# Second layer's q scaled inside its softmax, and its convolution, rotations and attention reordered on TensorE

## The chip, the cores and the metric

The kernel runs on one core of a Trainium2 chip. The metric is device time in microseconds (us) of one execution. A core has TensorE (PE, with its weight loads shown as PEld), VectorE (DVE), ScalarE (ACT), GpSimd (POOL), and the queue from which SyncE issues transfers (SP). Each engine works through its own list in order; semaphores tie the lists together.

## The reference, cut to what matters

Two transformer-like layers on 256 tokens of width 1024. The first has a recurrent unit, sparse attention and a dense feed-forward. The second, which the change touches, has differential attention and a long convolution side by side, then sixteen experts:

```python
q, k, v, hy, gts = jnp.split(proj, splits, axis=-1)        # 4 heads x 2 maps x 64
q = rope_partial(rms_norm_2(q, q_norm_g[li]), cos, sin)    # norm over each 64, then rotation
k = rope_partial(rms_norm_2(k, k_norm_g[li]), cos, sin)
# per head: pr = softmax(q k^T / 8), a = pr[map 0] - lam * pr[map 1], o = a v
o = rms_norm_2(o, subln_g) * (1.0 - lambda_init)           # norm over 128
# hyena: z = short_conv(hy) part; twice z = gate * (irfft(rfft(z) * spec) + skip * z)
merged = g_attn * (attn @ w_branch_attn) + g_hyena * (hyena @ w_branch_hyena)
x = x + merged @ w_out
x = x + expert_choice_ffn(rms_norm_2(x, norm2_g[li]), ...)  # each expert takes its 32 best tokens
```

The norm of q is a factor per token and per 64 channels. It commutes with the rotation, so it can be applied to the scores instead of to q.

## The kernel before

Activations lie with features on the partitions and the 256 tokens on the free axis; the products of the projections are fp32r products of high and low parts of weights and activations (`dense_split`, L463; `token_split`, L481), three products for each. A unit is a 2 MB block of weights, a half is 256 of its output columns. For each piece of weights (four to a half) ScalarE rounds the high part (`round_half`, L1203) and VectorE subtracts it for the low part (`rest_of_half`, L1589); four pieces have room at a time, so a piece can be rounded once TensorE has used the piece four before it. Thus while TensorE computes one half, ScalarE and VectorE prepare the next one.

The order of the work is written out by hand, once per engine. On TensorE, after the three units of the convolution input (L2 to L2+2): q (unit L2+3), k (L2+4), v (L2+5, token major), the gates (L2+6 to L2+9), with the rest between these halves. The names:

- `head_stats(i)` L517: one fp32 product that gives the mean square of each 64 channels, spread over all partitions, into bank 7. i = 6, 7 are the halves of q, 8, 9 those of k.
- `qk_half` L1394 (ScalarE): square, then the root of the means (`root_of`). `head_norm` L1882 (VectorE): `invert` L1558 (the reciprocal, L1561), product with norm weight and 1/root (L1885), product with the cosine (L1888).
- `rope(i)` L759: the permuting product into bank 7, which `finish_rope(i)` L1890 empties (product with the sine, L1892) before adding.
- `turn_hy` L764, `to_freq` L773, `to_time` L788: transposes of the convolution input, transform (m = 0, 1, two banks each), inverse transform. `multiply(o)` L1905 multiplies by the spectrum on VectorE (L1911 to L1923) for m = 0 and 1 in turn, and empties the two banks.
- attention, eight rounds a (head a // 2, query block a % 2): `att2_scores`, one half of the gates' `dense_split`, `att2_turn`, and for odd a `att2_out` and `sub_stats`. On VectorE `normalise2` L1950 takes the row maxima (L1953, L1954), waits for ScalarE's two exponentials (L1428) and normalises (L1956 to L1959). ScalarE then rounds pieces, empties the gates' bank (L1436), copies the transposed probabilities (L1440), squares the output (L1446) and takes a root (L1157) for the norm over 128; VectorE inverts it and scales (L1978).
- After the eight rounds: the branch products (units L2+10, L2+11), w_out, routing, and the loop of the experts.

In that loop, `expert block` semaphores (L956, L1078) let SP issue the load that refills an expert's slot; there are eight slots, and the first eight loads are issued ahead of it (`free`, L1064).

Of the kernel before, what the change touches and what calls it, by code (L numbers as in the profile page):

```python
# [20 lines left out]
ALU = mybir.AluOpType  # L21
# [3 lines left out]
P = 128  # L25
T = 256
# [96 lines left out]
def two_layers(nc, I, table, cols, out):  # L123
    with ExitStack() as ctx:
# [90 lines left out]
        xscale = small[:, 212:214]  # L215

# [57 lines left out]
        rot2 = area(14872, 512)  # L274
        prob2 = area(15872, 2, T)
# [140 lines left out]
        def _(pe):  # L416
# [356 lines left out]
            def to_freq(o, banks):  # L773

                for t in range(TT):
                    if o == 0:
                        wait_taken(("hy turn", 0, t))
                    else:
                        wait_taken(("hy time", 0, t))
                for m in range(2):  # L780
                    for part in range(2):
                        ps = take(banks[m][part], ("freq", o, m, part))
                        for t in range(TT):
                            c = part * T + m * P
                            last = mm(ps[:, :], fwd[:, t, c:c + P], ztok[:, t, :], t == 0, t == 1)
                        last.then_inc(S("freq"), 1)
# [16 lines left out]
            head_stats(6)  # L803
# [37 lines left out]
            def sub_stats(h):  # L841
                pe.wait_ge(S("out2 squares"), h + 1)
                ps = dense_bank(("sub", h))
                mm(ps[:, 0:T], mean_128, sqr[:, 0, 0:T]).then_inc(S("sub stats"), 1)

            halves = [(n, h) for n in range(L2 + 6, L2 + 10) for h in range(2)]
            for a in range(8):
                att2_scores(a)
                dense_split(*halves[a], 4)
                att2_turn(a)  # L850
                if a == 1:
                    to_freq(1, ((6, 7), (6, 7)))
                if a == 3:
                    to_time(1, (6, 7))
                if a % 2:
                    att2_out(a // 2)
                    sub_stats(a // 2)
# [4 lines left out]
            for h in range(4):  # L862
                wait_taken(("out2", h))
# [233 lines left out]
        def _(act):  # L1097
# [296 lines left out]
            def qk_half(i):  # L1394

                n, h = L2 + 3 + i // 2, i % 2
# [8 lines left out]
            qk_half(0)  # L1405
# [4 lines left out]
            qk_half(1)  # L1410
# [13 lines left out]
            for a in range(8):  # L1424
                h, q = a // 2, a % 2
                act.wait_ge(S("maxima2"), a + 1)
                for m in range(2):
                    ins = A(prob2[:, m, :], ps(("att2", a))[:, m * T:m * T + T], ACT.Exp, bias=nmx[:, m:m + 1],  # L1428
                            scale=SC1, accum_out=rsum[:, m:m + 1])
# [11 lines left out]
                if q:  # L1441
                    act.wait_ge(S("att2 out"), h + 1)
                    act.wait_ge(S("head stats"), 10)
                    if h:
                        act.wait_ge(S("sub stats"), h)
                    A(sqr[:, 0, 0:T], ps(("out2", h))[:, 0:T], ACT.Square).then_inc(S("out2 squares"), 1)  # L1446
                    root_of(("sub", h), T, "sub stats", h + 1)
# [48 lines left out]
        def _(dve):  # L1496
# [385 lines left out]
            def head_norm(i):  # L1882
                n, h = L2 + 3 + i // 2, i % 2
                invert(512, ("heads", 6 + i))
                X.scalar_tensor_tensor(rot, ps((n, h))[:, :], V("qn2" if i < 2 else "kn2"), rstd[:, :],  # L1885
# [4 lines left out]
            def finish_rope(i):  # L1890
                dve.wait_ge(S("rotated"), i + 1)
                empty(X.tensor_tensor(pair(rot), pair(ps(("rope", i))[:, :]), C("sin").unsqueeze(1).broadcast_to([P, 2, T]),  # L1892
                                      ALU.mult), ("rope", i))
                wait_taken(("rope", i))
                if i < 2:
                    X.tensor_tensor(q2[:, 2 * i:2 * i + 2, :], pair(rot), pair(rot2), ALU.add).then_inc(S("heads roped"), 1)
# [8 lines left out]
            def multiply(o):  # L1905

                for m in range(2):
                    zc, zs = ps(("freq", o, m, 0)), ps(("freq", o, m, 1))
                    pc, pz = spec[:, o, m, :], spec[:, o, 2 + m, :]
                    dve.wait_ge(S("freq"), 4 * o + 2 * m + 2)  # L1910
                    X.tensor_tensor(ya[:, m, :], zc[:, :], pc, ALU.mult)  # L1911
                    empty(X.tensor_tensor(ya[:, 2 + m, :], zc[:, :], pz, ALU.mult), ("freq", o, m, 0))
                    X.tensor_tensor(cross[:, 0, :], zs[:, :], pz, ALU.mult)
                    empty(X.tensor_tensor(cross[:, 1, :], zs[:, :], pc, ALU.mult), ("freq", o, m, 1))
                    wait_taken(("freq", o, m, 0))
                    wait_taken(("freq", o, m, 1))
                    minus = row0[:, 1:2] if m == 0 else -1.0
                    link(X.scalar_tensor_tensor(ya[:, m, :], cross[:, 0, :], minus, ya[:, m, :], ALU.mult, ALU.add))
                    link(X.tensor_tensor(ya[:, 2 + m, :], ya[:, 2 + m, :], cross[:, 1, :], ALU.add))
                    if m == 0:  # L1920
                        X.tensor_copy(ya[0:1, 2, :], cross[0:1, 0, :]).then_inc(S("products"), 1)
                    else:
                        X.tensor_copy(cross[:, 1, 0:8], cross[:, 0, 0:8]).then_inc(S("products"), 1)  # L1923
                    dve.wait_ge(S("products"), 2 * o + m + 1)

            rest_of_half(LATE + 15)
            head_norm(0)
# [22 lines left out]
            def normalise2(a):  # L1950
                h, q = a // 2, a % 2
                dve.wait_ge(S("att2 scores"), a + 1)
                link(X.tensor_reduce(mx[:, 0:2], pair(ps(("att2", a))[:, :]), AX.X, ALU.max))  # L1953
# [196 lines left out]
```

## Time and profile before

| | us |
|---|---|
| median of 3 runs | 1250.22 (1246.04 to 1253.16) |
| the profiled execution | 1249.02 |
| its span in the trace | 1247.1 |
| PE busy, of the span | 1136.6 (91%) |
| DVE busy | 509.0 (41%) |
| ACT busy | 399.1 (32%) |
| granted TensorE clock, mean | 0.969 |

The span is cut by the trace into a first layer and the inputs of the second (to 566), the stretch that the change rewrites (566.6 to 711.6), the branch products (to 739.4), w_out and routing (to 786) and the experts (to 1236), with a short end. A busy share of 91% says only that TensorE always has a product open; what a change is worth is read in its own stretch, from the time TensorE sat idle there, and from what the stages behind it wait for. In a line of the timeline the number in brackets is the idle time of the engine just before, and what ended it. Some starts of products overlap the modelled end of the one ahead, so a step is best read from start to start.

### The profile page before, as it was taken

To read this page: it belongs to the slowest core of one execution; us is meant where nothing else is said; L and a number is where in the kernel's file an instruction comes from. 1 tells how busy PE (TensorE), PEld (TensorE's weight loads), DVE (VectorE), ACT (ScalarE), POOL (GpSimd) and SP (SyncE) were. 2 spreads that over 40 slices of the span, in tenths; PEclk is the share of its full clock that TensorE was granted. 3 is DMA by queue.
4 is the path that set the end of the run, shared out by engine and by line. 5 is a ranking of instruction groups with operands and counts; after the bars stand their busy time and mean duration, and the time that the engine had idled before them with its cause. 6 is when DMAs were issued, how large, how long until landed. Compare 5 with 4: busy or idle time off the path is not lost.

```text
span 1247.1 us, 16271 instructions
## 1 busy us (share of the span) xinstructions
PE 1136.6 (91%) x6529; PEld 797.5 (64%) x6529; DVE 509.0 (41%) x970; ACT 399.1 (32%) x760; POOL 16.3 (1%) x28
## 2 busy tenths in 40 slices
PE   6999999999999999898899998798888887889886
PEld 5778989877899999896568887323232332323231
DVE  3357776585566655678856522200100010001001
ACT  2251665934656444564245602000000000000000
POOL 3000000000000000000000000000000000000000
PEclk8899999999999999899999999799999999999998
DMA  7163543333344667354122584499999999999997
GB/s 220 68 211 135 169 150 127 114 135 136 136 174 164 181 169 189 135 173 143 65 94 69 214 356 169 185 429 428 428 428 428 429 429 429 429 428 428 428 424 277
DMA packets 94059, 309.31 MB, mean 248 GB/s; under 512 B 6000, under 2 KB 39032, under 8 KB 82040
## 3 DMA queue, kind: packets, MB, share of 16 engines
q1 hardware_dynamic: 93256, 307.42, 64.0%
q0 software_dynamic: 496, 1.07, 0.4%
q8 instruction: 36, 0.59, 0.2%
q10 hardware_dynamic: 256, 0.10, 0.0%
q14 instruction: 15, 0.12, 0.0%
HBM read 307.53 MB, written 1.05 MB: 247 GB/s over the span
## 4 chain that ended last, share of the span: by engine, by line
PE 66%; DMA 26%; DVE 5%; ACT 1%; issue 1%; SPq 0%; ACTq 0%; DVEq 0%
PE bank L431 65%; DMA arena<-in_w_up 17%; DMA arena<-in_w_down 9%; DVE rstd L1561 1%; DVE parts L1589 1%; PE bank L638 0%; DMA arena<-in_x 0%; DVE arena L1524 0%; SPq L1084 0%; ACT root L1157 0%; DVE arena L1885 0%; DVE hidden_parts L1796 0%; DVE arena L1888 0%; ACT parts L1203 0%; DVE arena L1911 0%
## 5 line engine op out<-in xcount | busy, mean ns | idle before, releaser
L431 PE MATMUL bank<-arena 128*32 128x512 f32 (+6 forms) x724 | 268.4, 545 | 8.1 <-ACT arena L1492 3.0
L431 PE MATMUL bank<-parts 128*128 128x256 f32 (+1 forms) x1872 | 243.6, 291 | 5.0 <-DVE parts L1603 4.3
L431 PEld LDWEIGHTS bank<-parts 128*128 128x128 f32 x1872 | 232.9, 193 | 19.5 <-issue 16.5
L1589 DVE TENSOR_TENSOR parts<-ring,parts 128x512 fp32r<-128x512 f32 x288 | 193.0, 690 | 116.1 <-ACT parts L1203 114.8
L1203 ACT ACTIVATE parts<-ring 128x512 fp32r<-128x512 f32 x288 | 178.2, 628 | 189.5 <-PE bank L431 188.5
L431 PE MATMUL bank<-parts_room,arena 128*32 128x512 f32 x384 | 170.7, 634 | 20.5 <-DMA arena<-in_w_up 11.2
L431 PE MATMUL bank<-hidden_parts,parts 128*128 128x256 f32 x1024 | 164.9, 283 | 0.0
L431 PEld LDWEIGHTS bank<-hidden_parts,parts 128*128 128x128 f32 x1024 | 141.4, 192 | 0.1
L431 PEld LDWEIGHTS bank<-arena 128*32 128x32 f32 (+3 forms) x724 | 103.9, 174 | 40.2 <-issue 26.0
L2081 DVE TENSOR_TENSOR arena<-bank,arena 128x512 f32<-128x512 f32 x8 | 5.2, 686 | 279.8 <-ACT arena L1488 279.8
L431 PE MATMUL bank<-cst,arena 128*32 128x512 f32 (+2 forms) x226 | 97.0, 583 | 17.6 <-DMA arena<-in_w_gate 8.2
L431 PE MATMUL bank<-xh,arena 128*32 128x512 f32 (+1 forms) x224 | 94.1, 596 | 16.2 <-DMA parts_room<-in_w_up 8.2
L431 PE MATMUL bank<-xh_parts,parts 128*128 128x256 f32 x512 | 92.7, 283 | 0.6 <-DVE hidden_parts L1796 0.5
L431 PEld LDWEIGHTS bank<-parts_room,arena 128*32 128x32 f32 x384 | 39.5, 115 | 78.7 <-issue 72.4
L431 PE MATMUL bank<-ring,arena 128*32 128x512 f32 x384 | 84.7, 593 | 5.0 <-DMA ring<-in_w_gate 5.0
L431 PE MATMUL bank<-xh,ring 128*128 128x256 f32 x352 | 82.9, 397 | 1.3 <-DVE xh L1529 1.3
L431 PEld LDWEIGHTS bank<-xh_parts,parts 128*128 128x128 f32 x512 | 80.0, 192 | 1.0 <-DVE hidden_parts L1796 0.7
L431 PEld LDWEIGHTS bank<-xh,ring 128*128 128x128 f32 x352 | 70.3, 200 | 15.0 <-issue 4.7
L431 PEld LDWEIGHTS bank<-cst,arena 128*32 128x32 f32 (+2 forms) x226 | 26.9, 124 | 75.2 <-issue 73.2
L431 PEld LDWEIGHTS bank<-xh,arena 128*32 128x32 f32 (+1 forms) x224 | 24.3, 118 | 76.4 <-issue 74.0
L431 PEld LDWEIGHTS bank<-ring,arena 128*32 128x32 f32 x384 | 25.0, 110 | 57.3 <-issue 57.0
L1488 ACT ACTIVATE arena<-bank 128x512 f32<-128x512 f32 x8 | 4.3, 594 | 172.1 <-PE bank L431 172.1
(276 smaller groups left out, 925.6 us busy)
## 6 DMA issues: line engine op xcount, KB each, us to landing
ring<-in_w_in SPq DMA_DIRECT2D x22, 2048.0 KB, 7.9
ring<-in_w_gate SPq DMA_DIRECT2D x16, 2048.0 KB, 27.0
parts_room<-in_w_up SPq DMA_DIRECT2D x16, 2048.0 KB, 27.0
ring<-in_w_ff_in SPq DMA_DIRECT2D x8, 2048.0 KB, 8.5
ring<-in_w_ff_out SPq DMA_DIRECT2D x8, 2048.0 KB, 9.0
cst<-in_w_gate SPq DMA_DIRECT2D x8, 2048.0 KB, 22.7
arena<-in_w_gate SPq DMA_DIRECT2D x8, 2048.0 KB, 27.2
xh<-in_w_up SPq DMA_DIRECT2D x8, 2048.0 KB, 25.6
```

Source lines behind the costliest of these rows:

```text
L431: return nc.tensor.matmul(o, lhsT=l, rhs=r, start=first, stop=last)
L1203: A(w_part[0][:, p % PIECES], piece_of(n, p), ACT.Copy).then_inc(S("pieces rounded"), 1)
L1488: A(hs[:, 512 * h:512 * h + 512], bank[h][:, :], ACT.Silu).then_inc(emptied[h], 1)
L1561: X.reciprocal(rstd[:, 0:n], root[:, 0:n]).then_inc(S("rstd"), 1)
L1589: X.tensor_tensor(w_part[1][:, p % PIECES], piece_of(n, p), w_part[0][:, p % PIECES].bitcast(F32), ALU.subtract).then_inc(S("pieces split" ...
L2081: X.tensor_tensor(hh[:, 512 * h:512 * h + 512], bank[2 + h][:, :], hs[:, 512 * h:512 * h + 512], ALU.mult)\
```

## The change

Four things are done:

- **q is not normalised ahead of its rotation.** ScalarE copies q times the norm weight out of the bank (`q_half`), and VectorE's product with 1/root is gone for i = 0, 1. The mean squares of q are formed with tokens on the partitions (`q_stats`: four fp32 products of 2 columns for each half), their roots are 8 columns wide, and their reciprocals, times 1/8, are the scale of the softmax's exponentials and of its maxima.
- **The orders on TensorE** of turns, rotations, statistics and transforms change; `to_freq` and `multiply` are split by m and put at separate places, the last rotation goes behind `to_time(0)`.
- **In attention** the scores of round a + 1 are issued behind the turn of round a, and VectorE takes its maxima behind the pieces of weights of round a.
- **The norm over 128** is done for two heads at once (512 columns), after the fifth round and behind the first branch product; the outputs are first copied out of their banks by ScalarE.

```diff
             def rope(i):
                 wait_taken((L2 + 3 + i // 2, i % 2))
                 ps = take(7, ("rope", i))
-                mm(ps[:, :], C("perm"), rot).then_inc(S("rotated"), 1)
+                mm(ps[:, :], C("perm"), rot_q[:, i, :] if i < 2 else rot).then_inc(S("rotated"), 1)
+
+            def q_stats(i):
+
+                ps = take(7, ("q stats", i))
+                pe.wait_ge(S("head squares"), 7 + i)
+                for h in range(2):
+                    for t in range(TT):
+                        c = h * T + t * P
+                        last = mm(ps[:, 4 * h + 2 * t:4 * h + 2 * t + 2], sqr[:, i % 2, c:c + P], mean_64[:, 0:P:64])
+                last.then_inc(S("head stats"), 1)
...
             dense_split(L2 + 3, 0, 4)
-            head_stats(6)
             turn_hy(0)
             dense_split(L2 + 3, 1, 4)
             rope(0)
-            head_stats(7)
             turn_hy(1)
+            q_stats(0)
             dense_split(L2 + 4, 0, 4)
             rope(1)
+            to_freq(0, 0, (4, 5))
+            q_stats(1)
+            dense_split(L2 + 4, 1, 4)
             head_stats(8)
-            to_freq(0, ((4, 5), (4, 5)))
-            dense_split(L2 + 4, 1, 4)
-            rope(2)
-            head_stats(9)
-            token_split(L2 + 5, 4, lambda: rope(3))
+            to_freq(0, 1, (4, 5))
+
+            def between_values():
+                rope(2)
+                head_stats(9)
+
+            token_split(L2 + 5, 4, between_values)
             to_time(0, (5, 6))
+            rope(3)
 
             def att2_scores(a):
                 h, q = a // 2, a % 2
-                pe.wait_ge(S("heads roped"), 4)
+                pe.wait_ge(S("heads roped"), 3 + h // 2)
...
+            att2_scores(0)
             for a in range(8):
-                att2_scores(a)
                 dense_split(*halves[a], 4)
                 att2_turn(a)
-                if a == 1:
-                    to_freq(1, ((6, 7), (6, 7)))
+                if a < 7:
+                    att2_scores(a + 1)
+                if a % 2:
+                    att2_out(a // 2)
+                if a < 2:
+                    to_freq(1, a, (6, 7))
                 if a == 3:
                     to_time(1, (6, 7))
-                if a % 2:
-                    att2_out(a // 2)
-                    sub_stats(a // 2)
+                if a == 4:
+                    sub_stats(0)
             for t in range(2):
                 wait_taken(("hy time", 1, t))
             for h in range(4):
                 dense(L2 + 10, h, hyo, 4)
-            for h in range(4):
-                wait_taken(("out2", h))
+                if h == 0:
+                    sub_stats(1)
+            pe.wait_ge(S("att normed"), 2)
...
+            def q_half(i):
+
+                n, h = L2 + 3, i
                 act.wait_ge(*done((n, h)))
                 head_square(6 + i, ps((n, h))[:, :])
-                root_of(("heads", 6 + i), 512, "head stats", 7 + i)
+                empty(A(rot_q[:, i, :], ps((n, h))[:, :], ACT.Copy, scale=V("qn2")), (n, h))
+
+            def q_roots(i):
+                act.wait_ge(S("head stats"), 7 + i)
+                empty(A(q_root[:, 8 * i:8 * i + 8], ps(("q stats", i))[:, 0:8], ACT.Sqrt, bias=eps), ("q stats", i))
...
+            q_roots(0)
             round_half(LATE + 17)
-            qk_half(2)
+            k_square(2)
+            q_roots(1)
             round_half(LATE + 18)
-            qk_half(3)
+            k_square(3)
+            root_of(("heads", 8), 512, "head stats", 9)
             round_half(LATE + 19)
+            root_of(("heads", 9), 512, "head stats", 10)
             round_half(LATE + 20)
...
             rest_of_half(LATE + 15)
-            head_norm(0)
+            q_turned_by_cosine(0)
             dve.wait_ge(S("pads set again"), 2)
             rest_of_half(LATE + 16)
             finish_rope(0)
-            head_norm(1)
+            q_turned_by_cosine(1)
             rest_of_half(LATE + 17)
             finish_rope(1)
-            head_norm(2)
...
-            multiply(0)
+            multiply(0, 0)
+            for i in range(2):
+                wait_taken(("q stats", i))
+            link(X.reciprocal(q_scale, q_root))
+            link(X.tensor_scalar(q_scale, q_scale, SC1, None, ALU.mult))
             rest_of_half(LATE + 18)
+            k_norm(2)
+            multiply(0, 1)
+            rest_of_half(LATE + 19)
             finish_rope(2)
-            head_norm(3)
-            rest_of_half(LATE + 19)
-            finish_rope(3)
+            k_norm(3)
             rest_of_half(LATE + 20)
...
+            finish_rope(3)
...
+            maxima2(0)
             for a in range(8):
...
                 normalise2(a)
-                if a < 7:
-                    rest_of_half(LATE + 21 + a)
-                if a == 1:
-                    multiply(1)
-                if a == 3:
+                if a in (1, 2):
+                    multiply(1, a - 1)
+                if a == 4:
...
+                if a < 7:
+                    rest_of_half(LATE + 21 + a)
+                    maxima2(a + 1)
+                if a == 5:
+                    norm_heads(0)
+            norm_heads(1)
```

`k_norm(i)` is the old `head_norm(i)` for k; `q_turned_by_cosine(i)` is its product with the cosine alone. `maxima2` is the first half of the old `normalise2`, with `q_scale` in place of 1/8, and waits for the turn of the round before. `norm_heads(i)` inverts 512 roots and scales two heads in place.

## Rows read from the trace of the kernel before

**Rows 1.** The page: the chain that ended last, shares of the span by engine.

```profile
...
PE 66%; DMA 26%; DVE 5%; ACT 1%; issue 1%; SPq 0%; ACTq 0%; DVEq 0%
...
```

**Rows 2.** SP's queue from 690 us on: who it waited for: us in total, times, longest.

```profile
...
SPq L1084 <- PE bank L431: 431.0, 46, 26.8
...
```

**Rows 3.** Windows: length, busy (instructions) of PE, PEld, DVE, ACT, POOL, clock, DMA share, GB/s.

```profile
...
566.60:711.60 145.00, 129.68 (x745) 101.44 (x745) 98.35 (x157) 63.38 (x126) 0.00 (x0) 0.99 0.30 104
...
817.00:1236.00 419.00, 357.30 (x1599) 129.08 (x1598) 23.70 (x49) 22.47 (x38) 0.00 (x0) 0.96 1.00 426
...
595.90:600.80 4.90, 4.90 (x9) 2.12 (x9) 2.99 (x5) 0.00 (x0) 0.00 (x0) 0.65 0.00 0
...
```

**Rows 4.** TensorE's timeline, q to v: start, us, line, names, shapes, count, idle before.

```profile
...
559.75 6.88 PE L431 MATMUL bank<-parts 128*128 128x256 f32 x56
567.92 1.10 PE L431 MATMUL bank<-sqr,cst 128*128 128x512 f32 x2 [1.30 <-ACT sqr L1166]
568.86 1.04 PE L770 MATMUL bank<-cst,arena 128*128 128x128 f32 x8
569.65 6.00 PE L431 MATMUL bank<-parts 128*128 128x256 f32 x48
575.49 1.02 PE L431 MATMUL bank<-arena,cst 128*128 128x512 f32 x2
...
588.73 3.60 PE L431 MATMUL bank<-arena,cst 128*128 128x512 f32 x8
595.89 5.40 PE L431 MATMUL bank<-arena,cst 128*128 128x512 f32 x8 [3.57 <-DVE arena L1912]
...
616.61 5.76 PE L431 MATMUL bank<-parts 128*128 128x512 f32 x24
...
```

**Rows 5.** TensorE's timeline, attention and behind it.

```profile
...
622.21 7.03 PE L431 MATMUL bank<-arena,cst 128*128 128x512 f32 x16
629.07 1.02 PE L431 MATMUL bank<-arena 128*128 128x512 f32 x2
...
635.68 0.38 PE L829 MATMUL bank<-cst,arena 128*128 128x128 f32 x2
...
692.62 1.13 PE L431 MATMUL bank<-arena 128*128 128x256 f32 x4 [1.26 <-ACT arena L1440]
...
709.49 1.13 PE L431 MATMUL bank<-arena 128*128 128x256 f32 x4 [0.74 <-ACT arena L1440]
...
711.63 27.79 PE L431 MATMUL bank<-arena,ring 128*128 128x256 f32 x128
...
760.27 0.96 PE L431 MATMUL bank<-router,arena 128*128 128x16 f32 x8
...
```

**Rows 6.** VectorE's timeline.

```profile
...
569.78 3.35 DVE L1561 RECIPROCAL rstd<-root 128x512 f32<-128x512 f32 x1 [1.76 <-ACT root L1157]
...
574.68 2.50 DVE L1589 TENSOR_TENSOR parts<-ring,parts 128x512 fp32r<-128x512 f32 x4
...
594.55 0.69 DVE L1911 TENSOR_TENSOR arena<-bank,arena 128x512 f32<-128x512 f32 x1
...
598.65 0.42 DVE L1921 COPY arena<-arena 1x512 f32<-1x512 f32 x1
...
658.02 0.68 DVE L1953 TENSOR_REDUCE small<-bank 128x2 f32<-128x512 f32 x1
...
660.76 0.48 DVE L1959 SCALAR_TENSOR_TENSOR arena<-arena,small 128x256 f32<-128x256 f32 x1
...
```

**Rows 7.** ScalarE's timeline.

```profile
...
567.20 0.58 ACT L1166 ACTIVATE sqr<-bank 128x512 f32<-128x512 f32 x1
569.06 0.69 ACT L1157 ACTIVATE root<-bank,small 128x512 f32<-128x512 f32 x1 [1.28 <-PE bank L431]
...
652.71 1.28 ACT L1157 ACT_TABLE_LOAD   x1
654.00 0.47 ACT L1157 ACTIVATE root<-bank,small 128x256 f32<-128x256 f32 x1
...
```

More of the change, by code:

```diff
@@ L771, in turn_hy, with to_freq @@
                     last.then_inc(S("hy turned"), 1)
-            def to_freq(o, banks):
+            def to_freq(o, m, banks):
                 for t in range(TT):
[L776 to L786, printed above, removed]
+                    wait_taken(("hy turn", 0, t) if o == 0 else ("hy time", 0, t))
+                for part in range(2):
+                    ps = take(banks[part], ("freq", o, m, part))
+                    for t in range(TT):
+                        c = part * T + m * P
+                        last = mm(ps[:, :], fwd[:, t, c:c + P], ztok[:, t, :], t == 0, t == 1)
+                    last.then_inc(S("freq"), 1)
             def to_time(o, banks):
@@ L839, in att2_out, with sub_stats @@
                 last.then_inc(S("att2 out"), 1)
[L841 to L844, printed above, removed]
+            def sub_stats(i):
+                pe.wait_ge(S("out2 squares"), 2 * i + 2)
+                ps = dense_bank(("sub", i))
+                mm(ps[:, :], mean_128, sqr[:, i, :]).then_inc(S("sub stats"), 1)
             halves = [(n, h) for n in range(L2 + 6, L2 + 10) for h in range(2)]
+            att2_scores(0)
             for a in range(8):
-                att2_scores(a)
                 dense_split(*halves[a], 4)
                 att2_turn(a)
-                if a == 1:
-                    to_freq(1, ((6, 7), (6, 7)))
+                if a < 7:
[4 more added lines that the diff above has]
+                    to_freq(1, a, (6, 7))
                 if a == 3:
                     to_time(1, (6, 7))
-                if a % 2:
-                    att2_out(a // 2)
-                    sub_stats(a // 2)
+                if a == 4:
+                    sub_stats(0)
             for t in range(2):
@@ L1443, in _ @@
                     act.wait_ge(S("head stats"), 10)
[L1444 to L1447, printed above, removed]
+                    A(sqr[:, h // 2, (h % 2) * T:(h % 2) * T + T], ps(("out2", h))[:, 0:T], ACT.Square)\
+                        .then_inc(S("out2 squares"), 1)
+                    empty(A(att[:, h, :], ps(("out2", h))[:, 0:T], ACT.Copy), ("out2", h))
+                if a == 4:
+                    root_of(("sub", 0), 512, "sub stats", 1)
+            root_of(("sub", 1), 512, "sub stats", 2)
             for n, gates in ((L2 + 8, gates_h), (L2 + 6, gates_d)):
@@ L1891, in finish_rope @@
                 dve.wait_ge(S("rotated"), i + 1)
-                empty(X.tensor_tensor(pair(rot), pair(ps(("rope", i))[:, :]), C("sin").unsqueeze(1).broadcast_to([P, 2, T]),
+                r = rot_q[:, i, :] if i < 2 else rot
+                empty(X.tensor_tensor(pair(r), pair(ps(("rope", i))[:, :]), C("sin").unsqueeze(1).broadcast_to([P, 2, T]),
                                       ALU.mult), ("rope", i))
@@ L1903, in finish_rope @@
                 dve.wait_ge(S("heads roped"), i + 1)
[L1905 to L1924, printed above, removed]
@@ new lines, in multiply @@
+            def multiply(o, m):
+                zc, zs = ps(("freq", o, m, 0)), ps(("freq", o, m, 1))
+                pc, pz = spec[:, o, m, :], spec[:, o, 2 + m, :]
+                dve.wait_ge(S("freq"), 4 * o + 2 * m + 2)
+                X.tensor_tensor(ya[:, m, :], zc[:, :], pc, ALU.mult)
+                empty(X.tensor_tensor(ya[:, 2 + m, :], zc[:, :], pz, ALU.mult), ("freq", o, m, 0))
+                X.tensor_tensor(cross[:, 0, :], zs[:, :], pz, ALU.mult)
+                empty(X.tensor_tensor(cross[:, 1, :], zs[:, :], pc, ALU.mult), ("freq", o, m, 1))
+                wait_taken(("freq", o, m, 0))
+                wait_taken(("freq", o, m, 1))
+                minus = row0[:, 1:2] if m == 0 else -1.0
+                link(X.scalar_tensor_tensor(ya[:, m, :], cross[:, 0, :], minus, ya[:, m, :], ALU.mult, ALU.add))
+                link(X.tensor_tensor(ya[:, 2 + m, :], ya[:, 2 + m, :], cross[:, 1, :], ALU.add))
+                if m == 0:
+                    X.tensor_copy(ya[0:1, 2, :], cross[0:1, 0, :]).then_inc(S("products"), 1)
+                else:
+                    X.tensor_copy(cross[:, 1, 0:8], cross[:, 0, 0:8]).then_inc(S("products"), 1)
+                dve.wait_ge(S("products"), 2 * o + m + 1)
@@ L1960, in normalise2, with norm_heads @@
                     .then_inc(S("probs2"), 1)
+            def norm_heads(i):
+                invert(512, ("sub", i))
+                for h in (2 * i, 2 * i + 1):
+                    wait_taken(("out2", h))
+                pair_of = att[:, 2 * i:2 * i + 2, :]
+                X.scalar_tensor_tensor(flat(pair_of), flat(pair_of), lam[:, 5:6], rstd[:, :], ALU.mult, ALU.mult)\
+                    .then_inc(S("att normed"), 1)
+            maxima2(0)
             for a in range(8):
-                h, q = a // 2, a % 2
-                if a:
-                    dve.wait_ge(S("probs2 turned"), a)
                 normalise2(a)
-                if a < 7:
-                    rest_of_half(LATE + 21 + a)
-                if a == 1:
-                    multiply(1)
-                if a == 3:
+                if a in (1, 2):
+                    multiply(1, a - 1)
+                if a == 4:
                     for t in range(2):
```

39 lines of the change are left out of this document (23 added, 16 removed).

## The prediction

> **What bounds the kernel now.** First the chain that ended last [rows 1]: 66% of it is TensorE, 26% DMA. The DMA share all lies in the experts: from 817 to 1236 the DMA engines are busy all the time at 426 GB/s [rows 3], with TensorE waiting for them. But this stream has no clock of its own. SP's loads from 690 us on waited 46 times, 431 us in all, for TensorE [rows 2], since a load is issued when an expert block has used its slot. The first eight are ahead of the loop, the rest hang on its first block. So what TensorE saves ahead of the experts moves the stream and the end by as much, until the eight loads ahead become late.
>
> Ahead of the experts TensorE's own list is the bound. The stretch of the change begins where the first half of q ends (559.75 + 6.88 = 566.6 [rows 4]) and ends where the branch products begin, 711.6 [rows 5]: 145.0 us, in which TensorE is busy 129.7 [rows 3] and idle 15.3. This idle time is in a few gaps that the timeline shows with their releasers: 1.30 for the square of q, 3.57 for a bank that `multiply` holds [rows 4], 1.26 and 0.74 for the copies of the turned probabilities [rows 5], and others like them. VectorE and ScalarE are busy 98 and 63 us of the 145 [rows 3]: neither is the bound, but their order decides when a bank comes free.
>
> **The work on TensorE, step by step.** From start to start: a product of 512 fp32 columns 0.86 (eight in 622.21 to 629.07, the inverse transform [rows 5]), 0.95 where it stands alone (567.92 to 568.86 [rows 4]); eight turns 0.8 (to 569.65); a half with pieces 5.85 in q and k (to 575.49 [rows 4]) and 5.75 in attention (629.07 to 635.68 less a score of 0.86 [rows 5]); a half of v 5.7 (616.61 to 622.21 [rows 4, 5]); four products of `to_freq` 3.45. Thus, before: statistics 3.8, turns 1.6, rotations 3.6, `to_freq` 4 x 3.45 = 13.8, three halves 17.5, v 11.4, `to_time` 2 x 6.9 = 13.8, scores 8 x 0.86 = 6.9, gates 46.0, eight turns of 0.22 (an estimate from the eight in 0.8) 1.8, four outputs at 0.95 3.8, four norms of 256 columns at 0.53 (an estimate, half a 512 and a start) 2.1. Sum 126.1. So 145.0 - 126.1 = 18.9 us are not work: 15.3 idle, 1.4 in the second `to_freq` at half clock (below), and 2.2 in seams.
>
> **What is removed or made cheaper.** The q statistics become 8 products of 2 columns. The trace has no such product; the nearest row is the router's, 16 columns, 8 records (4 fp32 products) in 0.96 us [rows 5], where the stationary load is the cost. So four make 0.96 instead of 0.95: nothing. Bounds: 0.5 (only the records' starts) to 1.6 each, -0.9 to +1.3 for both. Two norms of 512 columns instead of four of 256: 1.9 for 2.1, one of them behind 711.6. VectorE loses two inversions of 3.35 [rows 6] and two products, gains two tiny ones; ScalarE has two copies of 0.6 for two roots of 0.7 [rows 7], and in attention two pairs of table loads instead of four.
>
> **The gaps after the change.** I write the lists out with these durations on the clock of the trace of before.
>
> q: the turns follow the first half at once (the 1.30 is gone), the second half runs 567.4 to 573.4, rotation and turns to 575.1. `q_stats(0)` needs bank 7 from `finish_rope(0)`, which is queued on VectorE behind four pieces; these end 1.7 after the half (577.2 against 575.49 [rows 4, 6]), so 575.1, and the sine product makes 575.8. Gap 0.7. k: `q_stats(0)` to 576.8, half to 582.6, rotation 583.5, first `to_freq` 587.0, `q_stats(1)` 587.9, half 593.8, `head_stats(8)` 594.7, second `to_freq` 598.2. Its banks were emptied long before, since `multiply(0, 0)` ran beside: the 3.57 and what hangs on it are gone. The first half of v to 603.9, `rope(2)` to 604.8.
>
> Then `head_stats(9)` needs bank 7 again, and I expect the largest new gap here. VectorE: pieces to 595.4; the root of `head_stats(8)` on ScalarE at 595.8 (behind a piece, the square 0.58 and 0.69 [rows 7]); inversion 3.35 and two products to 600.7; `multiply(0, 1)` 4.5 (594.55 to 599.07 [rows 6]) to 605.3; four pieces 2.5 to 607.8; sine product to 608.5. Gap 3.7. Queued behind this wait on TensorE are the second half of v, `to_time(0)`, all of attention.
>
> The clock: behind the idle 3.57 the granted clock was 0.65 on average in 595.9 to 600.8, where 3.45 us of products took 4.9 [rows 3, 4]; it fell to the 1.2 GHz level for some of it. I take the same 1.4 for the new gap of 3.7. Bounds 0 and 2.5 (half a clock over five us). The Trainium skill, "TensorE: Matmul & The Clock Gate", in "What's actually happening", says that an idle array goes to 1.2 GHz and that the moment varies between runs; by that the 1.4 could be missing in one execution with no change to the kernel. The row of this case shows only that it fell once.
>
> Attention: `rope(3)` and the first score wait for nothing. VectorE takes the maxima of round 0 at 626; softmax takes 3.2 (658.02 to 661.24 [rows 6]), done 1 us before the turn. In each later round the softmax follows TensorE's half by pieces 1.7, maxima 0.9, exponentials 1.1, normalising 1.3 = 5.0, while TensorE has turn, score and half, 6.8. So the turns wait for nothing, except round 6, behind the inversion of 512 (3.35): 0.2. `att2_out` waits for ScalarE's copy behind the gates' bank: 1.26 before in round 5, now less the score that lies in front of it, 0.4, in three rounds; in round 7, with no score, 0.74 [rows 5]. Together 2.0. The waits for the four squares and for `to_freq`'s second half are gone. Cover: were VectorE late, the next wait is that of the turn for the probabilities, at most 1 us away in rounds 0, 5 and 6. The last `norm_heads` ends about 5 us before the attention branch reads it, the gates' sigmoid about 3 us before its first bank is wanted; nothing.
>
> Sum after: gaps 0.7 + 3.7 + 1.4 + 2.0 + 0.2 = 8.0, seams 1.1 (half of 2.2, since half of those lay at banks that are now free; bounds 0.5 and 2.2) = 9.1 us instead of 18.9. With work less by 2.1 - 1.9 = 0.2 up to the end of the branch products (739.4 [rows 5]), they end 10.0 us earlier.
>
> **Does it arrive?** w_out's loads hang on the last gate half and move along; so do routing and the first expert block. 1249.0 (profiled, 1.9 beyond its span) - 10.0 = **1239.0 us**. That execution lies 1.2 under the median shown, so of the median 10 us would make 1240.2; I stay with the profiled one.
>
> **A rule weighed.** The root and the exponentials need different tables. The trace: load 1.28 at 652.71, root at 654.00, no pause [rows 7]. In round 4 the sequence score, `sub_stats`, root, load, exponentials leaves 0.4 us to the turn of round 5. The Trainium skill, "ScalarE: Activation LUTs", in "What ACT_TABLE_LOAD costs", gives 1.38 us of drain to each switch besides; by that the two switches would take 2.8 more, and the time would be 1239.0 + 2.4 = 1241.4. The rows speak against it.
>
> **Rivals.**
> 1. More comes: the gap at `head_stats(9)` stays under that which lowers the clock, seams vanish: 1239.0 - 1.4 - 1.6 = 1236. For it: the gap hangs on a chain of ten durations. Against: 3.57 lowered it once.
> 2. The thin margins break: the turns of rounds 0, 5, 6 and the second half of v each 1.5 late: +6, 1245. For: margins of 1 us and less. Against: each duration is read from a row.
> 3. The stream of the experts doesn't follow, because one of the eight loads ahead lands too late: 1249. Against: SP waited for TensorE 46 times and the DMA engines were idle before the loop.
> 4. The drains of the table loads: 1241.4.
> 5. Slower: the softmax, now behind the pieces of its own round on VectorE, becomes the chain of attention. It costs nothing up to 6.8 us a round. At 9.5 us it costs 8 x 2.7 = 21.6: 1260. It makes the kernel slower than before from 1.25 us a round over 6.8, slower by 0.5% from 2.0. Against: the sum is 5.0; for: a copy of the output and a square stand before the exponentials of even rounds, 5.9.
>
> **How the numbers follow.** Forecast 0.60, rival 1 0.12, rival 2 0.14, rival 3 0.05, rival 4 0.04, rival 5 0.05. The unknown costs reach from 1236 to 1242 in the forecast's own case. The range takes in rivals 1, 2 and 4 and the scatter of the runs (7 us between lowest and highest): 1233 to 1246; out are rivals 3 and 5, 0.10, and tails. A measurement of this kernel tells about 0.5%, 6.2 us, from no change: under 1244.0 counts as faster. Forecast, rivals 1 and 4 and a fifth of rival 2: 0.79. Same: the rest of rival 2, rival 3, a little of 5: 0.17. Slower 0.04.
>
> **What would show it.** In the profile after: no idle time before the turns at 566.6; under 1 us at `q_stats`; none at the second `to_freq`; one gap of 3 to 4 us inside v, released by the sine product, with a lower clock behind it; the branch products begin near 700.6; the first block of the experts 10 us earlier, the stream at the same rate. The prediction is wrong if that gap is over 8 us, or turns in attention wait for the probabilities in most rounds, or the products of 2 columns take over 0.3 us each.

## The result

The changed kernel takes 1236.22 us (median; 1233.94 to 1238.53), the kernel before 1248.95 in the same comparison (1246.04 to 1253.16): ratio 0.9897, 95% interval 0.9874 to 0.9921. That is 12.7 us less where 10.0 were forecast, and 2.8 under the forecast time of 1239.0, inside the range. The profiled execution of the changed kernel is its slowest, 1238.53, with a span of 1236.5; one thing that lengthened it is seen further down.

The page of the changed kernel, busy time and chain:

```profile
span 1236.5 us, 16274 instructions
...
PE 1136.0 (92%) x6537; PEld 800.6 (65%) x6537; DVE 500.8 (41%) x964; ACT 396.7 (32%) x760; POOL 16.3 (1%) x28
...
PE 67%; DMA 27%; DVE 3%; ACT 1%; issue 1%; SPq 0%; ACTq 0%; DVEq 0%
```

Over the whole span TensorE is busy nearly as long as before (1136.0 against 1136.6 us; this includes 2.4 us more in the last eight products, shown below), and VectorE's part of the chain went from 5% [rows 1] to 3%. In the rewritten part, from the end of q's first half to the first branch product, the window reads (length, busy of PE, PEld, DVE, ACT, POOL, granted clock, DMA share, GB/s):

```profile
566.60:698.80 132.20, 126.50 (x751) 101.89 (x750) 88.46 (x151) 59.73 (x123) 0.00 (x0) 0.99 0.32 111
```

TensorE sat idle 5.7 us there (132.2 - 126.5), and 15.3 before [rows 3]: most of what went is waiting. The timeline of TensorE, q to v (start, length, line, names, shapes, count, idle before):

```profile
566.43 1.04 PE L783 MATMUL bank<-cst,arena 128*128 128x128 f32 x8
567.22 6.00 PE L434 MATMUL bank<-parts 128*128 128x256 f32 x48
...
575.27 1.05 PE L434 MATMUL bank<-cst,sqr 128*128 128x2 f32 x8 [0.32 <-DVE arena L1930]
576.18 6.00 PE L434 MATMUL bank<-parts 128*128 128x256 f32 x48
582.02 4.45 PE L434 MATMUL bank<-arena,cst 128*128 128x512 f32 x10
586.31 0.95 PE L434 MATMUL bank<-cst,sqr 128*128 128x2 f32 x8
587.12 6.00 PE L434 MATMUL bank<-parts 128*128 128x256 f32 x48
592.96 1.02 PE L434 MATMUL bank<-sqr,cst 128*128 128x512 f32 x2
593.81 3.60 PE L434 MATMUL bank<-arena,cst 128*128 128x512 f32 x8
596.85 6.05 PE L434 MATMUL bank<-parts 128*128 128x512 f32 x24
602.73 1.02 PE L434 MATMUL bank<-arena,cst 128*128 128x512 f32 x2
607.19 1.83 PE L434 MATMUL bank<-sqr,cst 128*128 128x512 f32 x2 [3.44 <-DVE arena L1930]
608.04 7.38 PE L434 MATMUL bank<-parts 128*128 128x512 f32 x24
615.26 7.89 PE L434 MATMUL bank<-arena,cst 128*128 128x512 f32 x18
```

Against [rows 4]: the 1.30 and its like ahead of the statistics are gone but for 0.32, the second half of the transform (the 3.57 of before) follows without a bracket, and one gap is left, 3.44 us inside v. Attention and the branch products:

```profile
641.49 1.13 PE L434 MATMUL bank<-arena 128*128 128x256 f32 x4 [0.40 <-ACT arena L1471]
...
697.83 1.13 PE L434 MATMUL bank<-arena 128*128 128x256 f32 x4 [0.74 <-ACT arena L1471]
698.80 3.62 PE L434 MATMUL bank<-arena,ring 128*128 128x256 f32 x16
702.25 1.02 PE L434 MATMUL bank<-sqr,cst 128*128 128x512 f32 x2
703.11 24.34 PE L434 MATMUL bank<-arena,ring 128*128 128x256 f32 x112
```

The 0.40 stands in three rounds. I call the time from the end of q's first half to the first branch product the **stretch**. It was 145.0 us (566.6 to 711.6 [rows 4, 5]); it is 132.2 (566.6 to 698.8), 12.8 less. One norm of 0.86 now lies behind its end (702.25 to 703.11), so the branch products end 12.0 earlier, at 727.45 instead of 739.42 [rows 5].

### The profile page after: what moved, and what is told of

Same layout as the page of the kernel before. It is cut to its first block, busy times and chain, and to the rows that moved or that the text cites. A ratio compares the mean times of both kernels' runs of the same rounds, so it can differ in the third digit from the quotient of the medians.

```text
span 1236.5 us, 16274 instructions
## 1 busy us (share of the span) xinstructions
PE 1136.0 (92%) x6537; PEld 800.6 (65%) x6537; DVE 500.8 (41%) x964; ACT 396.7 (32%) x760; POOL 16.3 (1%) x28
## 4 chain that ended last, share of the span: by engine, by line
PE 67%; DMA 27%; DVE 3%; ACT 1%; issue 1%; SPq 0%; ACTq 0%; DVEq 0%
PE bank L434 66%; DMA arena<-in_w_up 17%; DMA arena<-in_w_down 9%; DVE parts L1622 1%; PE bank L641 0%; DVE rstd L1594 0%; DMA arena<-in_x 0%; DVE arena L1557 0%; SPq L1102 0%; DVE hidden_parts L1829 0%; ACT parts L1221 0%; PE bank L547 0%; PE bank L892 0%; ACT arena L1467 0%; DVE arena L2089 0%
```

## The experiments

Each kernel is read in two ways: its time beside the kernel before, with the ratio, and its stretch in the profile, which leaves out what varies ahead of it and behind.

**Which part gives the gain.** First the attention of the kernel before in the changed kernel (short: the lists of the three engines from the first score to the branch products).

```diff
-            att2_scores(0)
             for a in range(8):
+                att2_scores(a)
                 dense_split(*halves[a], 4)
                 att2_turn(a)
-                if a < 7:
-                    att2_scores(a + 1)
...
+                    sub_stats(a // 2)
```

> The changed kernel with the attention stretch of the kernel before: scores, half, turn in one round, all of the transform's second use behind round 1, four norms of 256 columns; q's scale stays in the softmax. Theory (the gain is the sum of TensorE's gaps, place by place, and nothing behind them gives it back): the attention stretch from the first score to the branch products goes back from 76.7 us (75.8 and the norm that lies behind) to 82.6, so 5.9 us more than the changed kernel, about 6 less than before: 1242, ratio 0.995. Rival (q's inversions out of VectorE's list are the gain, the order of attention is worth little): within 2 us of the changed kernel, 1236 to 1238.

Measured: 1247.27 us, ratio 0.9980 (0.9962 to 0.9998), stretch 142.0, so 9.8 more than the changed kernel where 5.9 and the 0.86 of the norm were expected. The timeline of TensorE shows a wait that neither kernel has:

```profile
607.18 1.90 PE L434 MATMUL bank<-sqr,cst 128*128 128x512 f32 x2 [3.43 <-DVE arena L1925]
625.37 1.12 PE L434 MATMUL bank<-arena 128*128 128x512 f32 x2 [2.20 <-DVE arena L1933]
644.20 3.67 PE L434 MATMUL bank<-arena,cst 128*128 128x512 f32 x8 [1.47 <-DVE arena L1944]
```

The old list waits for all four rotations ahead of the first score; the new list of q and k puts the last one behind the inverse transform. So I ran it again with the weaker wait:

```diff
-                pe.wait_ge(S("heads roped"), 4)
+                pe.wait_ge(S("heads roped"), 3 + h // 2)
```

> As the run with the old attention, but the first score waits only for the first half of k, as in the changed kernel. Theory (the 2.2 us by which that run lay beyond the sum of the gaps is a wait of the first score for the second half of k, whose rotation the new order puts behind the inverse transform): from the end of q's first half to the branch products 139.8 us instead of 142.0, no idle time ahead of the first score, and the two parts then add to the whole within 1 us. Rival (the old attention costs more on the new q and k for another reason, such as VectorE's list): 142 again.

Measured: 1242.65 us, ratio 0.9958 (0.9935 to 0.9982), stretch 139.5, no idle time ahead of the first score. The 2.2 us were that wait; the stretch is 2.5 shorter, since a wait costs more than its bracket (see below).

The other way round, the kernel before with the attention of the changed one:

> The kernel before with the attention stretch of the changed kernel only; q is normalised ahead of its rotation and everything up to the first score has the old order. Theory: TensorE's gaps up to the first score stay (8.8 idle and 1.4 of clock), those in attention go: 5.9 us less than before, 1243, ratio 0.995; with the other run the two parts add to the 12 us that the branch products gained. Rival (q's inversions are the gain): under 2 us less than before, ratio above 0.998.

Measured: 1242.17 us, ratio 0.9953 (0.9936 to 0.9969), stretch 138.3 (565.0 to 703.3): 6.8 less than before, of which 0.86 is the norm that lies behind; 5.9 as expected. The parts: 145.0 - 139.5 = 5.5 for q and k, 6.8 for attention, 12.3 of the 12.8 together. The rival falls: half of the gain has nothing to do with q. The place of the scores and the norm over two heads were only tested together.

**What scaling q in the softmax is worth.** The changed order, q normalised ahead of its rotation again:

```diff
             turn_hy(0)
+            head_stats(6)
             dense_split(L2 + 3, 1, 4)
             rope(0)
             turn_hy(1)
-            q_stats(0)
+            head_stats(7)
...
-            q_turned_by_cosine(0)
+            k_norm(0)
```

> The changed kernel's order, but q normalised ahead of its rotation: statistics spread over the partitions behind the turns of either half, root of 512, inversion of 512 and product with 1/root on VectorE, 1/8 alone in the softmax. Theory: VectorE has room for the two inversions in q and k, only the second statistics wait longer for bank 7 (gap 1.6 instead of 0.3): 1.3 to 1.6 us more than the changed kernel, 1238. Rival (the scaling in the softmax is what frees VectorE): 6 us or more above the changed kernel, 1242.

Measured: 1237.44 us (1232.90 to 1241.87), ratio 0.9911 (0.9877 to 0.9944), not to be told from the changed kernel. In its profile:

```profile
577.59 1.12 PE L434 MATMUL bank<-sqr,cst 128*128 128x512 f32 x2 [1.34 <-DVE arena L1929]
...
594.34 1.02 PE L434 MATMUL bank<-sqr,cst 128*128 128x512 f32 x2
...
608.57 1.13 PE L434 MATMUL bank<-sqr,cst 128*128 128x512 f32 x2 [3.43 <-DVE arena L1929]
609.13 6.05 PE L434 MATMUL bank<-parts 128*128 128x512 f32 x24
```

The first k statistics stand 28.0 us behind q's first half (566.4 to 594.3) instead of 26.4 (566.6 to 593.0): the 1.6 expected. But behind the gap of 3.43 the statistics and the second half of v take 6.45 (608.57 to 615.02) where the changed kernel takes 8.07 (607.19 to 615.26), and the stretch is 132.1. What this says of the clock comes below. The two inversions of 3.35 us that left VectorE are worth 1.6 us by the gaps, and in this profile the clock gave just as much back: the order gave the rest.

**What the split of the transform is worth.** Both of its halves behind the k statistics again:

```diff
             rope(1)
-            to_freq(0, 0, (4, 5))
             q_stats(1)
             dense_split(L2 + 4, 1, 4)
             head_stats(8)
+            to_freq(0, 0, (4, 5))
             to_freq(0, 1, (4, 5))
```

> The changed kernel with the first transform in one piece again: both halves of it behind the k statistics, and VectorE's two products behind the first inversion of k. Theory: TensorE waits 5 us at the second half for the banks that VectorE empties behind the inversion, with the clock at half behind it, and the gap at the last k statistics shrinks to 1: 4.4 us more than the changed kernel, 1240.6. Rival (the order within VectorE's list is indifferent, since it is busy 41%): no change.

Measured: 1240.68 us, 4.5 over the changed kernel, ratio 0.9938 (0.9918 to 0.9959); stretch 135.5, 3.3 more. That the medians lie as far apart as was forecast (4.4) is luck in part: by the stretch the forecast was 1.1 too large, since the wait was 3.81 and not 5. It is where it was forecast, with a smaller one at `q_stats(1)` and one at the last statistics (1.19):

```profile
583.02 1.05 PE L434 MATMUL bank<-cst,sqr 128*128 128x2 f32 x8 [1.19 <-DVE arena L1930]
598.03 5.37 PE L434 MATMUL bank<-arena,cst 128*128 128x512 f32 x8 [3.81 <-DVE arena L1949]
```

VectorE is busy 41% of the span, and the order within its list is still worth 3.3 us of the stretch.

**The gap that is left.** The last k statistics in bank 6, so that the sine product isn't waited for:

```diff
-            def head_stats(i, n=512):
+            def head_stats(i, n=512, b=7):
 
-                ps = take(7, ("heads", i))
+                ps = take(b, ("heads", i))
...
                 rope(2)
-                head_stats(9)
+                head_stats(9, b=6)
```

> The changed kernel, the last k statistics in bank 6 instead of bank 7, so that they needn't wait for the sine product. Theory: the gap of 3.44 us inside v shrinks to about 0.25 (the pieces of the second half of v are ready at 604.7), the clock stays at full behind it (1.3 us), and nothing else is late: 4.8 us less than the changed kernel, 1231.4. Rival (the clock's dip has nothing to do with the gap): 3.2 us less and the dip still there. Rival (VectorE's chain is next: the second inversion and the pieces behind it are late): the gap moves behind v and under 1 us is gained.

Measured: 1232.12 us, 4.1 less than the changed kernel by the medians (four executions, two near 1229.5 and two near 1234.8), ratio 0.9876 (0.9829 to 0.9924). The stretch is 127.3 (565.3 to 692.6), 4.9 less, as expected. The gap is 0.17, then:

```profile
603.45 5.73 PE L434 MATMUL bank<-parts 128*128 128x512 f32 x24 [0.17 <-DVE parts L1622]
609.02 7.88 PE L434 MATMUL bank<-arena,cst 128*128 128x512 f32 x18
```

Next, ScalarE's copies in the other order, besides:

```diff
+                act.wait_ge(S("probs2 turned"), a + 1)
+                if q == 0 and h:
+                    act.wait_ge(S("att2 out"), h)
+                empty(A(aT[:, :, q * P:q * P + P], ...), ("turn2", a))
                 act.wait_ge(*done((n, hh_)))
                 dst = (gates_d if a < 4 else gates_h)[:, 2 * (a % 4):2 * (a % 4) + 2, :]
                 empty(A(dst, pair(ps((n, hh_))[:, :]), ACT.Copy), (n, hh_))
```

> The last k statistics in bank 6, and on ScalarE the copy of the turned probabilities ahead of the copy out of the gates' bank. Theory: besides the 4.8 us of bank 6, the waits of the attention outputs go (0.40 in three rounds, and 0.4 of the 0.74 in the last): 6.2 to 6.4 us less than the changed kernel, 1230, which would beat both. Rival (the turn of the next round then waits for the probabilities instead, since their margin in rounds 5 and 6 was 0.3 and 0.1): 4.8 less.

Measured: **1229.86 us** (1228.43 to 1232.29), ratio 0.9853 (0.9808 to 0.9897); stretch 126.1, 6.1 less than the changed kernel. The three waits of 0.40 are gone and the 0.74 is 0.47; in round 6 the turn now waits 0.37 for the probabilities. By its median this version lies 6.4 under the changed kernel and is the fastest here; the run with bank 6 alone is not told from it by its interval, only by the stretch (1.2 longer).

And the sine product ahead of the pieces instead:

```diff
             multiply(0, 1)
-            rest_of_half(LATE + 19)
             finish_rope(2)
+            rest_of_half(LATE + 19)
```

> The changed kernel, with VectorE's sine product and additions of k's first half ahead of the four pieces of weights for the second half of v instead of behind them. Theory: the one gap of 3.44 us becomes two of 1.2 us, ahead of the k statistics and ahead of the second half of v, and the clock does not fall: 2.7 us less than the changed kernel, 1233.5. Rival (the clock goes by the sum of idle time in the stretch): the dip stays, 1.3 less.

Measured: 1235.35 us where 1233.5 was expected, ratio 0.9893 (0.9848 to 0.9938), stretch 131.1, 1.2 less than the changed kernel instead of 2.7. The two gaps came (1.02 each), but the clock fell all the same. TensorE's timeline, and windows (length, busy of PE, PEld, DVE, ACT, POOL, granted clock, DMA share, GB/s):

```profile
606.03 1.13 PE L434 MATMUL bank<-sqr,cst 128*128 128x512 f32 x2 [1.02 <-DVE arena L1930]
608.18 7.36 PE L434 MATMUL bank<-parts 128*128 128x512 f32 x24 [1.02 <-DVE parts L1622]
...
608.00:610.00 2.00, 1.82 (x5) 1.45 (x6) 1.93 (x4) 0.00 (x0) 0.00 (x0) 0.69 0.00 0
610.00:612.00 2.00, 2.00 (x6) 1.60 (x5) 1.98 (x1) 0.63 (x1) 0.00 (x0) 0.50 0.48 65
```

My expectation for the clock failed here; the rival's 1.3 came. The next run asks whether one gap as long as these two together does it too.

```diff
             multiply(0, 1)
+            link(X.reciprocal(cross[:, 0, 0:256]..., mean_d...))
             rest_of_half(LATE + 19)
```

> The run with bank 6 for the last k statistics, and one more reciprocal of 256 columns (1.75 us) on VectorE ahead of the pieces for the second half of v; its result is not used. Theory (idle time makes the clock fall even when it is spread or short of 3 us, as in the run with two gaps of 1.0): one gap of 1.9 us ahead of the second half of v and half clock behind it, 3.0 us more in the stretch than with bank 6 alone, 130.3. Rival (a gap of 1.9 leaves the clock alone, and the other run fell for the product between its gaps): 1.75 more, 129.0, granted clock 1.00 throughout.

Measured: 1236.78 us in one execution, stretch 130.7, 3.4 more than with bank 6 alone, gap 1.96, clock 0.50 behind it:

```profile
606.00:608.00 2.00, 2.00 (x6) 1.55 (x5) 1.97 (x4) 0.34 (x1) 0.00 (x0) 0.50 0.04 9
```

**How much room attention has.** A reciprocal whose result is not used, 1.75 us, ahead of the maxima of each round:

```diff
                     rest_of_half(LATE + 21 + a)
+                    link(X.reciprocal(rot2[:, 0:256]..., mean_d...))
                     maxima2(a + 1)
```

> The changed kernel with one more reciprocal of 256 columns (1.75 us) on VectorE ahead of the maxima in rounds 1 to 7; its result is not used. Theory (margins differ from round to round, and the delays of rounds 1 and 2 add up ahead of the pieces for round 3): 2.2 at the pieces of round 3, 1.4 at its turn, nothing in round 4, 1.5, 1.7 and 0.6 in rounds 5 to 7: 7.4 us more from the first score to the branch products. Rival (the softmax is the chain of every round): 12.3 us more. Rival (VectorE is not near a bound in attention): 0 to 2.

Measured: 1239.67 us in one execution, stretch 136.0, 3.8 more instead of 7.4. TensorE waited for the probabilities in rounds 3, 6 and 7:

```profile
658.69 0.44 PE L843 MATMUL bank<-cst,arena 128*128 128x128 f32 x2 [0.90 <-DVE arena L2005]
...
691.74 0.44 PE L843 MATMUL bank<-cst,arena 128*128 128x128 f32 x2 [1.67 <-DVE arena L2005]
...
699.26 0.44 PE L843 MATMUL bank<-cst,arena 128*128 128x128 f32 x2 [0.48 <-DVE arena L2005]
```

I had counted 2.2 for late pieces in round 3 and 1.5 in round 5; the first was 0.4, the second nothing. Both rivals (12.3 and 2) fall. All brackets of the attention together grew by 3.1, and the clock behind them stayed at 1.00. Then twice the delay:

> The changed kernel with one more reciprocal of 512 columns (3.35 us) on VectorE ahead of the maxima in rounds 1 to 7, twice the delay of the earlier run, whose stretch grew by 3.8 us; its result is not used. Theory (margins are used up one after the other, so cost grows faster than delay): each 1.6 us more goes fully into rounds 3, 5, 6 and 7, where the smaller delay had already used up the margin, and rounds 1 and 2 delay the pieces of round 3: 10 to 13 us more than the changed kernel, 142 to 145. Rival (cost in proportion): 7.3 more, 139.5.

Measured: 1248.89 us in one execution, the gain gone; stretch 145.6, 13.3 more. The largest new waits are the one for the pieces of round 3 and the one of round 6's turn for its probabilities:

```profile
656.49 8.40 PE L434 MATMUL bank<-parts 128*128 128x256 f32 x48 [3.60 <-issue]
...
700.47 0.69 PE L843 MATMUL bank<-cst,arena 128*128 128x128 f32 x2 [3.58 <-DVE arena L2005]
...
701.88 8.32 PE L434 MATMUL bank<-parts 128*128 128x256 f32 x48
```

So 1.75 us a round cost 3.8 and 3.35 cost 13.3: cost grows faster than delay. But the used-up margins are only part of it. The brackets of the attention grew by 7.3 us here, 2.4 times the 3.1 of the smaller delay, for 1.9 times the delay. Behind each of the two long waits the granted clock was 0.50 (656 to 662 and 700 to 706): the half of round 3 took 8.40 us where it took 5.99 behind the shorter wait, and round 6's turn, score and next half took 2.7 more as well. These 5.1 us of clock I had not counted. Nor did rounds 5 and 7 pay as I had written: 0.48 and nothing. The total, just over my upper end of 13, is near for another reason than the one I gave.

## Why the prediction held, and where it missed

**The stretch, term by term.** Forecast: gaps and clock 8.0, seams 1.1. Measured in the changed kernel:

| term | forecast | measured |
|---|---|---|
| `q_stats(0)` for bank 7 | 0.7 | 0.32 |
| `head_stats(9)` for bank 7 | 3.7 | 3.44 |
| the clock behind it | 1.4 | 1.6 (8.07 less 6.45, statistics and half of v, start to start, against the run that normalised q ahead) |
| `att2_out` for ScalarE's copy | 2.0 | 1.94 |
| round 6 | 0.2 | about 0.1 |
| seams | 1.1 | nothing: 132.2 less the 7.4 above and less the work, which the forecast's count puts at 125.0 up to there, is -0.2 |

The last chain was written down as ten durations on VectorE and ScalarE, and came out 0.26 us long. Bounding the gap by a list of steps, each with its row, was enough; no term needed a row that the trace of before lacks, except the products of 2 columns, forecast at 0.96 and measured at 0.91 and 0.81 (575.27 to 576.18, 586.31 to 587.12). The range of 0.5 to 1.6 for them was far too wide.

**The step that was mis-sized** is the seams: "seams 1.1 (half of 2.2, since half of those lay at banks that are now free; bounds 0.5 and 2.2)". By the forecast's count of the work none are left, but the timeline shows that they are not gone. A seam is what a wait costs beside its bracket: the product ahead counts 1.02 where the next one would start after 0.86, and the first product behind takes 1.13 instead of 1.02, about 0.25 together. The stretch had 13 such waits and has 6, so by this estimate 1.8 us of seams went and 1.5 stayed, and the work was counted too large by about as much. One such place is the half of v, put at 5.7: 593.81 to 602.73, less four products in 3.45, makes 5.5. So of the 12.0 us at the end of the branch products 9.6 are idle time (15.3 to 5.7) where 8.7 were forecast (15.3 to 6.6), and 2.4 are seams and cheaper work where 1.3 were. The forecast's clock term was too small in the kernel before as well: there 10.98 us (595.89 to 606.87) stand against 9.18 for the same products without a wait (630.66 to 639.84 in the changed kernel), 1.7 and not 1.4 once 0.1 for the first product behind a wait is taken off.

**Does it arrive?** Yes, and the experts' stream follows rigidly. SP's first load behind the eight ahead, in the kernel before and the changed one:

```profile
800.66 0.33 SPq L1084 DMA_DIRECT2D cst<-in_w_gate  x1
```

```profile
787.03 0.33 SPq L1102 DMA_DIRECT2D cst<-in_w_gate  x1
```

It is 13.6 us earlier, 1.6 more than the branch products, because the clock rose sooner at the first block (0.67 in the kernel before from 786 to 800, 0.85 here from 774 to 788). Its first four pairs of products start 0.83 apart before (791.96 to 795.29) and 0.43 apart here (779.93 to 781.65), which makes the 1.6. The lead is kept through the stream, and partly lost at its end. The chain of waits, the two last pieces on TensorE before the last sum, before and after:

```profile
1236.24 3.30 PE bank L431 x16
...
1240.22 3.71 PE bank L431 x8
```

```profile
1222.83 3.68 PE bank L434 x16
...
1227.19 6.15 PE bank L434 x8
```

The last eight products took 6.15 us instead of 3.71, at half clock:

```profile
1226.00:1230.00 4.00, 3.29 (x8) 1.27 (x5) 1.38 (x2) 0.60 (x1) 0.00 (x0) 0.50 0.00 0
```

With the same code there, they take 6.1 in four other profiles too (q normalised ahead, the joined transform, the first run with the old attention, the gap of 1.96) and 3.7 in the remaining eight, that of the kernel before among them; no run shows what decides it. So the spans differ by 10.6 us and the medians by 12.7; the stretch says 12.0. The forecast was one for the profiled execution, and two errors, a gain 2.0 too small and a clock that I couldn't foresee, nearly cancelled in it (1238.5 against 1239.0). That it came this close is luck.

**The rivals.** "More comes" is half right: 2.0 more came, but not by a clock that stayed up; 0.9 of it is shorter waits. The thin margins (rival 2) held, by little: the probabilities of round 5 were done 0.3 us before their turn. The delays of the last two runs put a price on them. The softmax as the chain of attention (rival 5) was to make the kernel slower than before from 1.25 us a round over 6.8, a delay of 3.05 on a chain of 5.0; a delay of 3.35 gave a stretch of 145.6, that of before. That the point is about right is luck: 5.1 of those 13.3 us are the clock, and the waits lie in rounds 3 and 6, while round 4 pays nothing.

**The table loads (rival 4).** ScalarE's timeline of the changed kernel, round 4:

```profile
675.35 1.28 ACT L1175 ACT_TABLE_LOAD   x1
676.64 0.69 ACT L1175 ACTIVATE root<-bank,small 128x512 f32<-128x512 f32 x1
677.35 1.28 ACT L1459 ACT_TABLE_LOAD   x1
678.64 0.56 ACT L1459 ACTIVATE arena<-bank,small 128x256 f32<-128x256 f32 x1
```

Each switch costs 1.28 us, and the next activation starts 0.01 behind it. The Trainium skill, "ScalarE: Activation LUTs", in "What ACT_TABLE_LOAD costs", gives the same 1.28 and a drain of 1.38 besides; this trace has no such drain, and had it been there, the turn of round 5 would have waited over 2 us. It didn't wait.

**What I had not asked.** The prediction priced the gaps and never the parts. It left open which of the four edits pays. The runs say: the attention's order with its norms 5.9 and the norm's place 0.86, the split transform 3.3, q's scale 1.6 by the gaps and nothing that the times can tell.

What stays open: the parts add to 12.3 of 12.8, and I have no row for the last 0.5. Nor does any run show why the smaller delay cost less in rounds 3 and 5 than I had written down.

## What to carry to other kernels

Where one engine holds the end, write its gaps down with their releasers, lay the new lists of the other engines on the same clock with durations from rows, and look for whoever holds the next bank: the sum was right to 2 us in 145. A change with a clever part and a dull reordering should be priced in parts, because here the dull part paid. The largest gap that such a ledger forecasts is the next edit; a free bank for one product gave 4.9 us more.

## What the runs showed of the hardware

The granted clock falls to its 1.2 GHz level after shorter and more scattered idle time than I had thought, and not every time. Gaps of 1.3 us ten us apart left it at 1.00 in the kernel before, and a gap of 2.20 left it at 1.00 in the first run with the old attention. One gap of 1.96, and two of 1.02 with one product between, were each followed by 0.50. So the length of the gap alone doesn't decide. Windows of the first run with the old attention (its 2.20), and of the changed kernel behind its 3.44:

```profile
622.00:626.00 4.00, 1.80 (x6) 0.59 (x4) 2.75 (x4) 0.00 (x0) 0.00 (x0) 1.00 0.00 0
```

```profile
608.00:610.00 2.00, 2.00 (x5) 1.30 (x4) 0.77 (x2) 0.69 (x1) 0.00 (x0) 0.50 0.87 311
```

The same gap of 3.4 us in the same place was followed by 0.50 in the changed kernel and in the four other profiles with its order and its scaling of q up to there, and cost 1.6 us in each (8.07 to 8.10 for statistics and half of v). It cost nothing in the run that normalised q ahead:

```profile
610.00:612.00 2.00, 2.00 (x10) 1.65 (x9) 1.54 (x1) 1.06 (x2) 0.00 (x0) 1.00 1.00 379
```

The Trainium skill, "TensorE: Matmul & The Clock Gate", in "What's actually happening", says that the point of the transition varies; it gives the spread for the rise to full speed, which no run here measures. Whether the one exception here is such a variation of the fall, or comes of the other list of q ahead of it, is open, since there is one profile of that run. For a ledger this means that a gap like these carries 0 to 1.6 us which its length doesn't settle.
